# Attention scores, maxima and sums: one subtraction per step, one reduction per bank pair, one sum moved

## The reference, cut to what matters

```python
def diff_attend(q, k, v, lam):
    s = jnp.einsum('bqhmd,bkhmd->bhmqk', q, k).astype(F32) * (DA_QK ** -0.5)
    p = jax.nn.softmax(s, axis=-1)
    w = p[:, :, 0] - lam * p[:, :, 1]
    return jnp.einsum('bhqk,bkhv->bqhv', w, v)
```

## Time and profile before

| | |
|---|---|
| runs of the kernel before, us | 5883.33 median of 3 (5879.26 to 5887.54) |
| profiled execution, span, us | 5891.0 |
| mean granted clock of PE, share of full speed | 0.947 |
| busy share of the span: PE, DVE, POOL, ACT | 93%, 50%, 39%, 29% |
| attention of layer 0, of layer 1, from the start, us | about 2070 to 2720, about 4920 to 5620 |

### The profile page before, as it was taken

The page is one execution under the profiler, slowest core; times in us unless marked ns, Lnnn a source line. Parts: engine busy times, 40 slices in busy tenths (PEclk is TensorE's granted clock), DMA queues, the critical chain, the costliest instruction groups (busy, mean ns, idle before and its releaser), DMA issues. The chain is left out here.

```text
span 5891.0 us, 74540 instructions
## 1 busy us (share of the span) xinstructions
PE 5465.5 (93%) x26120; PEld 2879.7 (49%) x26120; DVE 2921.8 (50%) x4926; ACT 1691.0 (29%) x4067; POOL 2311.5 (39%) x1695
## 2 busy tenths in 40 slices
PE   5999999978988899998989999999678879999989
PEld 2445445436777533332445544544467763333334
DVE  1445544544777655551113455455557766555312
ACT  1111111112334244444002212212223433444421
POOL 0112212113444289998001112111234434999910
PEclk7999999976999899999999999999779998999999
DMA  6233233257222100000633333333462210000032
GB/s 239 88 105 98 98 105 98 94 171 232 97 81 97 54 1 8 8 6 9 244 112 107 100 100 102 100 99 97 140 205 82 97 59 34 1 8 8 4 129 86
DMA packets 356833, 530.61 MB, mean 90 GB/s; under 512 B 89488, under 2 KB 233672, under 8 KB 350128
## 3 DMA queue, kind: packets, MB, share of 16 engines
q1 hardware_dynamic: 330754, 453.12, 23.1%
q10 hardware_dynamic: 19728, 40.41, 1.8%
q0 software_dynamic: 6048, 33.11, 1.6%
HBM read 372.13 MB, written 154.08 MB: 89 GB/s over the span
## 5 line engine op out<-in xcount | busy, mean ns | idle before, releaser
L607 PE MATMUL psum<-group_W,projection_hT 128*128 128x512 f32 (+4 forms) x5016 | 1953.8, 546 | 5.9 <-DVE projection_hT L729 5.7
L607 PEld LDWEIGHTS psum<-group_W,projection_hT 128*128 128x128 f32 x5016 | 949.2, 191 | 974.4 <-issue 932.7
L2277 POOL TENSOR_TENSOR attention_PS<-attention_PS 128x1024 f32<-128x1024 f32 x548 | 1265.8, 2354 | 81.9 <-ACT attention_PS L2410 73.7
L2323 DVE TENSOR_REDUCE attention_mxp<-psum 128x1 f32<-128x512 f32 (+1 forms) x1016 | 654.3, 686 | 541.0 <-PE psum L2460 541.0
L459 POOL TENSOR_TENSOR projection_cx<-projection_cx,projection_cw 128x768 f32<-128x768 f32 x102 | 188.0, 1843 | 1686.4 <-DMA projection_cw<-in_ss_conv_w 1686.4
L2410 ACT ACTIVATE attention_PS<-psum 128x512 f32<-128x512 f32 (+1 forms) x1168 | 630.6, 592 | 717.6 <-PE psum L2514 690.8
L2460 PE MATMUL psum<-attention_QK 32*128 32x512 f32 (+1 forms) x2592 | 772.9, 616 | 8.7 <-DVE attention_mxp L2312 5.8
L2508 PE MATMUL psum<-attention_QK 32*128 32x512 f32 x2336 | 664.4, 642 | 0.0
L2526 PE MATMUL psum<-attention_PS,attention_va 128*64 128x512 f32 x2336 | 627.7, 616 | 0.0
L680 ACT ACTIVATE projection_ut<-psum 128x256 f32<-128x256 f32 (+2 forms) x322 | 127.3, 406 | 1420.4 <-PE psum L607 1408.0
L782 DVE TENSOR_SCALAR projection_e<-projection_e 128x256 f32<-128x256 f32 (+1 forms) x170 | 60.1, 353 | 843.4 <-ACT projection_e L692 843.4
(11 more groups left out here) (366 smaller groups left out, 6242.0 us busy)
## 6 DMA issues: line engine op xcount, KB each, us to landing
u<-projection_ut SPq DMA_DIRECT2D x240, 256.0 KB, 2.0
projection_cx<-xbc SPq DMA_DIRECT2D x306, 128.0 KB, 2.2
projection_cw<-in_ss_conv_w SPq DMA_DIRECT2D x102, 384.0 KB, 4.4
mixing_hg<-u SPq DMA_DIRECT2D x34, 1024.0 KB, 5.0
group_W<-in_w_in SPq DMA_DIRECT2D x8, 2316.0 KB, 18.9
output_y<-y SPq DMA_DIRECT2D x34, 512.0 KB, 4.7
group_W<-in_w_in POOLq DMA_DIRECT2D x6, 2316.0 KB, 28.9
xbc<-projection_ut SPq DMA_DIRECT2D x34, 384.0 KB, 2.4
```

Of the source, the lines that this page charges most:

```text
L607: ins = nc.tensor.matmul(ps[n % RING][:, lo - c0:lo - c0 + w], hT[b][:, q], W[q][:, lo:lo + w], start=(q == 0), stop=(q == KT - 1))
L2277: G.tensor_tensor(SA[x % 2][:, rs, 0:w], one[:, rs, 0:w], PT[i % PTB][:, rs, 0:w], ALU.add) \
L2323: bk.release(V.tensor_reduce(mxp[x % 2][:, q:q + nn, 2 * pr + j, a], bk[job, j][:, 0:nn * (hi - lo)].rearrange("p (q n) -> p q n", q=nn), ...
```

## The change

It makes four edits in the attention stage. (1) The subtraction of the maxima is done for the four banks of a step together, in pass 1, and the values of the step before stand between the two passes' score jobs: the order on PE is scores 0, maxima, values 0, scores 1, maxima, subtraction of all four, values 1. ACT's four exponentials follow that one subtraction. (2) The two banks of a maxima job are taken, filled, reduced by one instruction and released together. (3) The running sum of the fourth map (r = 3) moves from POOL to DVE, with a semaphore of its own; POOL's second addition has one map instead of two. (4) The turn of the maxima goes to the end of its slot, on PE and on ACT, and its place in the order of the banks with it; the copies of the collected values on ACT stand ahead of the exponentials of their maps.

```diff
@@ -2141,12 +2141,13 @@
                 u = next(pair)
                 uses += [(("st", i, 2 * p + j), u + j) for j in range(2)]
             if mx[i][p]:
-                uses += [((mx[i][p], j), 6 + j) for j in range(2)]
-            if p == 0 and i in turn:
-                uses.append((("turn", turn[i]), next(pair)))
+                uses.append((mx[i][p], 6))
+        if i in turn:
+            uses.append((("turn", turn[i]), next(pair)))
         uses += [(job, next(pair)) for job in extras[i]]
     parts = [(0, CT + QG)] + [(t, min(t + 4, NT)) for t in range(CT + QG, NT, 4)]
-    added = [2 * (i - x + (n == 0)) for i, (x, n) in enumerate(steps)]
+    fourth = [i - x + (n == 0) for i, (x, n) in enumerate(steps)]
+    added = [2 * n for n in fourth]
     finish = {last[2 * g + 1] + 8: g for g in range(NG)}
     prologue = [(q, a, pr) for a in range(5) for q in range(QG) for pr in range(2)]
 
@@ -2180,7 +2181,7 @@
         oneb = k.sb(c, "oneb", [P, P], BF16)
         ones = k.sb(c, "ones", [P, DQ])
         s = k.sems(c, "consts_in memsets x_in1 x_in2 x_in3 v_in key_mm key_copied pro_mm pro_read "
-                      "dve_step act_step pool_step lam_dot lam_exp ready mneg_ready mm_ready pv_done added acc_free sq_ready "
+                      "dve_step act_step pool_step lam_dot lam_exp ready mneg_ready mm_ready pv_done added fourth_added acc_free sq_ready "
                       "ssq_ready rstd_ready out_ready z_in0 z_in1 stored0 stored1")
         bk = Turns(k, c, uses)
 
@@ -2264,8 +2265,8 @@
                         x, n = steps[i]
                         w = groups[halves[x][0]][1] * P
                         for pr in range(2):
-                            rs = slice(2 * pr, 2 * pr + 2)
-                            for r in (2 * pr, 2 * pr + 1):
+                            rs = slice(2 * pr, 2 + pr)
+                            for r in ((0, 1), (2,))[pr]:
                                 if n == 1:
                                     bk.freed(gp, ("st", i - 1, r))
                                 bk.freed(gp, ("st", i, r))
@@ -2299,8 +2300,7 @@
                 def maxima(x):
                     nq, n = groups[halves[x][0]][1], len(groups[halves[x][0]][3])
                     if x:
-                        for j in range(2):
-                            bk.freed(dve, (end[x], j))
+                        bk.freed(dve, end[x])
                         dve.wait_ge(s["mm_ready"], x)
                     V.tensor_reduce(mneg[:, 0:nq], mxp[x % 2][:, 0:nq, :, 0:n], AX.X, ALU.max, negate=True) \
                         .then_inc(s["mneg_ready"], 1)
@@ -2318,11 +2318,29 @@
                 def maximum(job):
                     x, q, nn, a, pr = job[1:]
                     lo, hi = groups[halves[x][0]][3][a]
-                    for j in range(2):
-                        bk.wait(dve, (job, j))
-                        bk.release(V.tensor_reduce(mxp[x % 2][:, q:q + nn, 2 * pr + j, a],
-                                                   bk[job, j][:, 0:nn * (hi - lo)].rearrange("p (q n) -> p q n", q=nn),
-                                                   AX.X, ALU.max), (job, j))
+                    bk.wait(dve, job)
+                    banks = k.psum[:, 512 * bk.bank[job]:512 * bk.bank[job] + 1024].rearrange("p (r n) -> p r n", r=2)
+                    if nn == 1:
+                        ins = V.tensor_reduce(mxp[x % 2][:, q, 2 * pr:2 * pr + 2, a], banks[:, :, 0:hi - lo], AX.X, ALU.max)
+                    else:
+                        ins = V.tensor_reduce(mxp[x % 2][:, q:q + nn, 2 * pr:2 * pr + 2, a].rearrange("p q r -> p r q"),
+                                              banks[:, :, 0:nn * (hi - lo)].rearrange("p r (q n) -> p r q n", q=nn), AX.X, ALU.max)
+                    bk.release(ins, job)
+
+                def fourth_added(i):
+
+                    x, n = steps[i]
+                    w = groups[halves[x][0]][1] * P
+                    if n == 1:
+                        bk.freed(dve, ("st", i - 1, 3))
+                        if x >= 2:
+                            bk.wait(dve, ("sm", x - 2))
+                    else:
+                        dve.wait_ge(s["fourth_added"], fourth[i] - 1)
+                    bk.freed(dve, ("st", i, 3))
+                    one = PT[(i - 1) % PTB] if n == 1 else SA[x % 2]
+                    V.tensor_tensor(SA[x % 2][:, 3, 0:w], one[:, 3, 0:w], PT[i % PTB][:, 3, 0:w], ALU.add) \
+                        .then_inc(s["fourth_added"], 1)
 
                 def sums(job):
                     x = job[1]
@@ -2354,9 +2372,11 @@
                     bk.release(ins, job)
 
                 for i in SLOTS:
-                    for job in mx[i]:
+                    for p, job in enumerate(mx[i]):
                         if job:
                             maximum(job)
+                        if p == 0 and 0 < i <= len(steps) and steps[i - 1][1]:
+                            fourth_added(i - 1)
                     for x in due.get(i, []):
                         maxima(x)
                     for job in extras[i]:
@@ -2399,19 +2419,24 @@
                     A(AS[x % 2][:, j, 0:w], k.bank[4 + j][:, 0:w], ACT.Copy).then_inc(s["acc_free"], 1)
 
                 for i in SLOTS:
-                    for p in range(2):
-                        if 0 <= i < len(steps):
-                            w = groups[halves[steps[i][0]][0]][1] * P
-                            if i >= PTB:
-                                act.wait_ge(s["pv_done"], 2 * (i - PTB) + 1 + p)
-                                act.wait_ge(s["added"], added[i - PTB] - 1 + p)
-                            for r in (2 * p, 2 * p + 1):
-                                bk.wait(act, ("st", i, r))
-                                bk.release(A(PT[i % PTB][:, r, 0:w], bk["st", i, r][:, 0:w], ACT.Exp, scale=scale), ("st", i, r))
-                        if p == 0 and i in turn:
-                            turned(turn[i])
-                        if i - 1 in last:
-                            accumulated(steps[i - 1][0], p)
+                    if i - 1 in last:
+                        accumulated(steps[i - 1][0], 0)
+                    for r in range(RG):
+                        if r == 2 and i - 1 in last:
+                            accumulated(steps[i - 1][0], 1)
+                        if not 0 <= i < len(steps):
+                            continue
+                        w = groups[halves[steps[i][0]][0]][1] * P
+                        if i >= PTB:
+                            if r % 2 == 0:
+                                act.wait_ge(s["pv_done"], 2 * (i - PTB) + 1 + r // 2)
+                                act.wait_ge(s["added"], added[i - PTB] - 1 + r // 2)
+                            if r == 3:
+                                act.wait_ge(s["fourth_added"], fourth[i - PTB])
+                        bk.wait(act, ("st", i, r))
+                        bk.release(A(PT[i % PTB][:, r, 0:w], bk["st", i, r][:, 0:w], ACT.Exp, scale=scale), ("st", i, r))
+                    if i in turn:
+                        turned(turn[i])
                     for job in extras[i]:
                         if job[0] == "sm":
                             x = job[1]
@@ -2489,28 +2514,28 @@
                 def maximum(job):
                     x, q, nn, a, pr = job[1:]
                     lo, hi = groups[halves[x][0]][3][a]
+                    bk.take(pe, job)
                     for j in range(2):
-                        bk.take(pe, (job, j))
                         for i in range(nn):
-                            ins = scored(bk[job, j], x, q + i, a, 2 * pr + j, i * (hi - lo))
-                        bk.done(ins, (job, j))
+                            ins = scored(k.bank[bk.bank[job] + j], x, q + i, a, 2 * pr + j, i * (hi - lo))
+                    bk.done(ins, job)
 
                 def scores(i, p):
                     x, n = steps[i]
                     t0, nq, kts, chunks = groups[halves[x][0]]
                     a0 = halves[x][1]
-                    if n == 0:
-                        bk.freed(pe, ("turn", x))
                     kt = kts[n]
                     for r in (2 * p, 2 * p + 1):
                         bk.take(pe, ("st", i, r))
                         o_ = bk["st", i, r][:, 0:nq * P]
                         T(o_, QK[rows(r), 2 + a0, kt * P:(kt + 1) * P], QK[rows(r), a0, t0 * P:(t0 + nq) * P], start=True, stop=False)
 
-                def shifted(i, p):
+                def shifted(i):
                     x, n = steps[i]
                     nq = groups[halves[x][0]][1]
-                    for r in (2 * p, 2 * p + 1):
+                    if n == 0:
+                        bk.freed(pe, ("turn", x))
+                    for r in range(RG):
                         bk.done(T(bk["st", i, r][:, 0:nq * P], oneb[DQ * r:DQ * r + 3, :], MT[x % 2][DQ * r:DQ * r + 3, 0:nq * P],
                                   start=False, stop=True), ("st", i, r))
 
@@ -2531,6 +2556,7 @@
```

(9 more changed lines are left out.)

## The result

The changed kernel takes 6025.0 us (median of four runs, 6021.1 to 6033.9) against 5883.3 before (median of three runs; a fourth took 10084.2 us and is left out): slower, at a ratio of 1.0243 (95% interval 1.0227 to 1.0258), 142 us. The forecast was 6064, 181 us more, with a range from 5960 to 6115. In what follows a *half* is always the 18 steps of one pair of heads; the two parts of a step are called passes.

What follows compares the result with a forecast made beforehand. PE's own work was taken to set the attention stage's pace, POOL hidden just behind. Steps with maxima 155 us, extra jobs 18, steps without maxima 2, blocks before step 0 6: 181 on 5883 gives 6064 us, range 5960 to 6115.

Steps and rivals of the forecast that it cites:

- The bank pair's loop: Banks 6 and 7: blocks' start to reduction 1.18, reduction 1.21, release to PE's next load 0.07; 2.46 us per pass.
- The late bank of map 1: PE's score of map 1 waits for ACT's exponentials; it and pass 0's maxima go about 1.70 us after the subtraction starts.
- The regular step: Attention step with maxima, both bank waits together, no DVE and POOL collision: grows from 4.60 to 5.13 us.
- The tie of DVE and POOL: DVE's addition meets POOL's changeover: mean step 5.34 us if POOL goes first, 5.13 if DVE does; middle 5.23 taken.
- Extra jobs: Five jobs per half (turn of maxima, sums, their turn, two heads): 0.98 us each instead of 0.76, 18 us in all.
- Steps without maxima: The 21 attention steps per layer without maxima blocks: 4.63 us instead of 4.58, 2 us in all.
- Blocks before step 0: Six maxima blocks before step 0, at the low clock, 2.85 us each: later release adds 0.53 each, 6 us in all.
- Values between the passes: Values placed between the two passes' score jobs: their inputs are ready over 1 us early, so they cost nothing.
- POOL's relief: Fourth map's sum off POOL: its work falls to 3.6 us a step, but it did not bound the step; brings nothing.
- rival 3: PE's granted clock falls in a third of the attention stage, some 100 to 200 us more: 6200 us; chance 0.04.
- rival 1: Attention: only the bank pair 6 and 7 binds, 2.46 us per pass, ACT's banks return earlier: 5968 us; chance 0.16.
- rival 2: Attention: PE's saved 0.31 us a step is all that counts, 91 us go: 5792 us; chance 0.09.

Runs made afterwards that it cites:

- run 1: The kernel before, with only the two banks of a maxima job taken, reduced and released together: 5937.7 us, 1.0095.
- run 9: The changed kernel with the maxima block of pass 0 placed between the scores of maps 0 and 1: 5993.6 us, 1.0188.
- run 4: The changed kernel with the fourth map's sum back on POOL: 6023.5 us, 1.0244.
- run 3: The changed kernel with maxima banks taken, reduced and released one by one, the addition still on DVE: 5986.8 us, 1.0176.
- run 2: The changed kernel with separate maxima banks and all sums on POOL, keeping one subtraction, values between passes and later turn: 5984.2 us, 1.0172.
- run 7: The kernel of run 2 with pass 1 reordered: block of bank 6, subtraction of maps 0, 2, 3, block of bank 7, subtraction of map 1: 5950.1 us.

## Why the prediction was right, and where it was off

- **The bank pair's loop**: 2.46 forecast, 2.47 in the changed kernel, 2.46 in runs 1 and 9. Shown.
- **The late bank of map 1**: blocks of pass 0 forecast 1.70 after a subtraction that starts 0.97 after the blocks, 2.67 in all; measured 2.60. Shown by run 9. Its inside was not what I wrote. The subtractions are not 0.4 together but 0.78: maps 2 and 3, whose row groups are free, start at 2402.62, and maps 0 and 1 behind their blocks about 0.4 later; ACT starts 0.49 after the latter, for which I had taken 0.53.
- **The regular step**: 5.13 without a collision, measured 5.07: 246 x 0.06 = 15 us too much.
- **The tie of DVE and POOL**, "I take the middle, 5.23": the term that was mis-sized most. It was priced as if half of the steps lost 0.21. Of the 274 additions 184 took under 1.1 us (0.68 at 2401.92, in a step of 5.07) and 82 more than 1.5, up to 2.8, with a mean of 1117 ns: the collision is real, but most steps have room for it. In the half from 2446.5 one step was 6.06 behind an addition of 2.55, in the half before it two were 5.38 and 5.20. The term was 25 us; run 4 finds 1.5 by the medians and 11 in the attention time.
- **Extra jobs**, 0.98 each: the exponentials behind one are 6.05 apart, 5.07 + 0.98. Right:

```profile
2465.84 2.06 ACT L2437 ACTIVATE attention_PS<-psum 128x512 f32<-128x512 f32 x4 [3.00 <-PE psum L2539]
...
2471.88 2.06 ACT L2437 ACTIVATE attention_PS<-psum 128x512 f32<-128x512 f32 x4 [3.49 <-PE psum L2539]
2477.93 2.06 ACT L2437 ACTIVATE attention_PS<-psum 128x512 f32<-128x512 f32 x4 [3.98 <-PE psum L2539]
```

- **Steps without maxima**, 4.63 against 4.58: wrong in sign, 4.46 (ACT starts at 5651.93 and 5656.39). I had let the subtraction of all four begin when the last scores were through; maps 0 and 1 are subtracted beside the scores of maps 2 and 3. It is worth 42 x 0.17 = 7 us.
- **Blocks before step 0**: 3.38 forecast at the low clock, 3.40 measured (2055.56 to 2058.96, granted clock 0.50).
- **The sum**: 181 less 15, 7 and 14 to 24 for the tie leaves 135 to 145; 142 was measured. All three errors point the same way.
- **Values between the passes**: nothing, as forecast, as far as the trace shows; it was not tried alone. **POOL's relief**: nothing, as forecast, and runs 3 and 4 show it.
- **The clock** stayed at 1.00 over the five halves; rival 3 falls, and rivals 1 and 2 with the step of 5.07.
- Of the signs to look for, four failed. Halves are 97.05 and not 98 to 100, and the four subtractions take 0.78 and not 0.4, as said above. PE does not fall below 90%: it is busy 481 of 485 us, since records of matmuls in other row groups cover the waits. And DVE's reduction is named as the releaser of the blocks' loads only 19 times, because the wait stands beside running scores. The starts of the blocks showed it, not the busy time.

Alone, the joined bank pair costs 55 us, the one subtraction 102 and the moved sum 17, in all 174; together they cost 142. They overlap: with joined banks the two blocks of pass 1 start together (2407.13), the exponentials start 1.45 after them and not 1.70, and the 0.25 of run 2 is not paid. Run 2 has the later turn of the maxima and the values between the passes in it too, which were not tried alone. No version of this study is faster than the kernel before. The gain of 0.31 a step on PE would need the four banks free again when PE comes back, and with eight banks in use they are not; this is read from the timelines, no run had more banks. In the steps without maxima 0.12 of it was had (4.46 for 4.58).

## What to carry to other kernels

Where one engine writes a bank and another reads it, count the loop of the bank, not the busy time of the engines: write, latency, read and release must fit in the period, and giving two banks back together puts both reads in that loop. Merging instructions of the fullest engine can cost more than they take if the merge makes the results come late and all at once. Moving work to an idle engine pays nothing while the relieved engine is not the bound.

## What the runs showed of the hardware

A matmul's end reached ScalarE in program order, even where its record ended earlier. (The profile models the ends of PE's records, so the conclusion rests on the starts of two runs.) In run 2 map 0's subtraction ended at 2402.25 by its record and the exponential started at 2402.61, 0.15 after the end of a block ahead of it in the program; with the block moved behind it (run 7) the exponential started 0.25 sooner at the same starts of the records. In the changed kernel's steps without maxima the same is seen:

```profile
5650.66 0.70 PE L2531 MATMUL psum<-attention_QK 32*128 32x512 f32 x2
5650.68 0.39 PE L2539 MATMUL psum<-attention_MT,attention_oneb 3*128 3x512 bf16 x2
...
5651.20 0.59 PE L2531 MATMUL psum<-attention_QK 32*128 32x512 f32 x2
5651.63 0.38 PE L2539 MATMUL psum<-attention_MT,attention_oneb 3*128 3x512 bf16 x2
5651.93 2.06 ACT L2437 ACTIVATE attention_PS<-psum 128x512 f32<-128x512 f32 x4 [2.40 <-PE psum L2539]
```

By the records, the first two subtractions ended at 5651.07, the scores ahead of them in the program at 5651.79, and the exponentials started at 5651.93. Starts, on the other hand, were not in program order: there and at 2402.62 a subtraction in a free row group started before what stood ahead of it in another. The Trainium skill, TensorE: Matmul & The Clock Gate, section "Packing small matmuls — row/col tiling", says that matmuls end in program order; the ends as ACT sees them agree, the starts do not agree with the same sentence's order of starts.
